# Gates and output projection of a hybrid decoder layer as seven block products in place of eight, token-major

## The chip, the core and the metric

The kernel runs on one core of one Trainium2 chip. The metric is the time of one execution on the device, in microseconds (us). The core has five engines that run side by side, each through its own list of instructions in order: TensorE (PE in the rows, with its weight loads as PEld), VectorE (DVE), ScalarE (ACT), GpSimd (POOL) and SyncE (SP), which here only issues DMA transfers. They wait for one another on semaphores. SBUF is the memory beside the engines, PSUM the eight banks that TensorE writes to.

## What is computed

One layer on 512 tokens of 2048 channels, all in float32. The parts that matter here:

```python
h = _rmsnorm(x, norm_g[l])
proj = jnp.einsum('bsd,df->bsf', h, w_in[l])      # 2048 x 24576
parts = jnp.split(proj, SPLIT_POINTS, axis=-1)
...                                               # attention A, attention B, short convolution C
gates = jax.nn.sigmoid(parts[9 + 3 * n_g] + gate_b[l]).reshape(bsz, seq, N_BRANCH, D_MODEL)
...
merged = (gates[:, :, 0] * jnp.einsum('bsw,wd->bsd', ya, w_branch_a[l])
          + gates[:, :, 1] * jnp.einsum('bsw,wd->bsd', yb, w_branch_b[l])
          + gates[:, :, 2] * jnp.einsum('bsw,wd->bsd', yc, w_branch_c[l]))
x = x + jnp.einsum('bsd,de->bse', merged, w_out[l])
return _rmsnorm(x, final_g)
```

18 x 1024 of the columns of `w_in` feed the three branches, the last 6144 the gates. `ya`, `yb`, `yc` are 1024 wide; `w_out` is 2048 x 2048.

## The kernel before

Everything lies channel-major in SBUF: 128 channels on the partitions, the 512 tokens along them. A weight **unit** is 128 x 1024 floats (512 KB): eight 128 x 128 blocks. TensorE multiplies in a rounded float32 format (fp32r), so each operand is split in a high part (`w_hi`, `act_hi`) and what is left (`w_lo`, `act_lo`), and a product is three matmuls (`three`, L329): high by high, low by high, high by low. A unit is thus 8 x 3 = 24 matmuls of a 128 x 128 stationary block of weights against 128 x 512 of activations, accumulated in one PSUM bank (`multiply`, L335).

The units pass through a ring of three slots. SyncE loads `raw[slot]` when the low part that was made from the slot before is done (semaphore `lo_done`); ScalarE copies it to `w_hi[slot]` (`split_hi`, L571), for which TensorE must have finished the unit three places earlier (`pe_used`); VectorE subtracts to get `w_lo[slot]` (`split_lo`, L811); TensorE waits for `lo_done` (L499 to L530). The order of the work is written out by hand: each engine's program says between which units its other instructions stand.

Four stages: the heads (8 heads x 36 units of `w_in`, with the attention and convolution work of that head between units; `y` of each branch is stored to DRAM); the merged columns (16 columns, each of six gate units and three branch units, `merge_block`, L499, `merge`, L1034), which are stored to DRAM, too; the output projection (16 blocks of two units, `out_block`, L525), the result read out of PSUM and added to `x` by `add_residual` (L1094); and the final norm, whose sum over channels is a sum over partitions, so it goes through GpSimd and two small turns on TensorE (L542 to L560) before all 16 blocks are scaled and stored.

Units: 288 + 96 + 48 + 32 = 464, so 464 x 24 = 11136 large matmuls.

## Time and profile before

| | |
|---|---|
| time of 3 runs | median 2722.65 us, 2722.07 to 2724.84 |
| the profiled execution | 2723.15 us, span 2721.4 us, mean granted clock of TensorE 0.997 |
| TensorE busy | 2690.2 us (99%) |
| VectorE, ScalarE, GpSimd busy | 1223.5 us (45%), 764.1 us (28%), 25.7 us (1%) |
| chain that ended last | TensorE 96%, VectorE 2%, DMA 1%, ScalarE 1% |
| DMA | 278.64 MB, mean 102 GB/s |

The rows come from one profiled execution. A row of the timeline gives start, duration, engine, line, operation, output<-inputs and shapes; the bracket is how long the engine stood idle before it and what ended that. Matmuls overlap: each row shows 0.39 us, but the next one starts 0.23 us later, so it is the distance of the starts that counts. The same holds by some tenths for VectorE and ScalarE.

### The profile page before, as it was taken

What the parts mean: (1) busy time and instruction counts of PE and PEld (TensorE: products, weight loads), DVE (VectorE), ACT (ScalarE), POOL (GpSimd) and SP (SyncE); (2) the same over time, 40 slices, a digit from 0 to 9 for tenths busy, and PEclk for the clock granted to TensorE, in tenths of its full rate; (3) what the DMA queues carried; (4) which work ended last, traced back from release to release, by engine and by line L of the source; (5) the groups of instructions that cost most, each with busy time, mean ns of one, the idle gap of its engine ahead of it and who ended that gap; (6) DMA issues with size and microseconds to landing.
All of it is one profiled execution on the core that took longest, in us unless ns stands there. A gap on an engine that the chain in (4) does not pass through costs nothing.

```text
span 2721.4 us, 32865 instructions
## 1 busy us (share of the span) xinstructions
PE 2690.2 (99%) x12330; PEld 2225.3 (82%) x12330; DVE 1223.5 (45%) x1613; ACT 764.1 (28%) x973; POOL 25.7 (1%) x23
## 2 busy tenths in 40 slices
PE   8999999999999999999999999999999999999997
PEld 6888888888888888888888888878888888888786
DVE  6554553554554455454455455443333333333323
ACT  5222322322232232232222232332222222223332
POOL 0000000000000000000000000000000000000011
PEclk9999999999999999999999999999999999999998
DMA  5222222222222222222222322443233333233532
GB/s 183 89 86 101 88 90 99 93 89 94 93 89 93 93 91 87 97 96 83 97 89 87 100 91 90 143 141 107 97 103 101 104 100 104 96 108 120 189 100 93
DMA packets 85119, 278.64 MB, mean 102 GB/s; under 512 B 9121, under 2 KB 9378, under 8 KB 85026
## 3 DMA queue, kind: packets, MB, share of 16 engines
q1 hardware_dynamic: 75472, 259.56, 28.7%
q10 hardware_dynamic: 9554, 17.63, 1.7%
q8 instruction: 83, 1.36, 0.2%
q14 instruction: 10, 0.08, 0.0%
HBM read 262.74 MB, written 14.42 MB: 102 GB/s over the span
## 4 chain that ended last, share of the span: by engine, by line
PE 96%; DVE 2%; DMA 1%; ACT 1%; issue 0%; DVEq 0%; ACTq 0%; SPq 0%
PE proj L331 30%; PE proj L333 30%; PE proj L332 30%; PE tr_ps L372 2%; PE sc_ps L364 1%; DMA raw<-wst 1%; PE o_ps L417 1%; PE sc_ps L403 1%; DMA raw<-y_dram 0%; DVE res L1120 0%; DVE y_lo L817 0%; PE o_ps L332 0%; PE o_ps L333 0%; PE o_ps L331 0%; PE sc_ps L332 0%
## 5 line engine op out<-in xcount | busy, mean ns | idle before, releaser
L331 PE MATMUL proj<-act_hi,w_hi 128*128 128x512 f32 x3328 | 1308.1, 393 | 10.9 <-DVE act_lo L826 8.7
L333 PE MATMUL proj<-act_hi,w_lo 128*128 128x512 f32 x3328 | 1297.3, 390 | 0.0
L332 PE MATMUL proj<-act_lo,w_hi 128*128 128x512 f32 x3328 | 1296.0, 389 | 0.0
L813 DVE TENSOR_TENSOR w_lo<-raw,w_hi 128x1024 fp32r<-128x1024 f32 x464 | 568.5, 1226 | 1001.8 <-ACT w_hi L575 1001.4
L575 ACT ACTIVATE w_hi<-raw 128x1024 fp32r<-128x1024 f32 x464 | 491.1, 1059 | 1404.9 <-PE proj L333 1383.4
L331 PEld LDWEIGHTS proj<-act_hi,w_hi 128*128 128x128 f32 x3328 | 625.5, 188 | 138.3 <-issue 11.7
L333 PEld LDWEIGHTS proj<-act_hi,w_lo 128*128 128x128 f32 x3328 | 625.2, 188 | 132.4
L332 PEld LDWEIGHTS proj<-act_lo,w_hi 128*128 128x128 f32 x3328 | 625.8, 188 | 126.5
L331 PE MATMUL proj<-y_hi,w_hi 128*128 128x512 f32 x384 | 150.0, 391 | 1.8 <-DVE y_lo L817 1.8
L332 PE MATMUL proj<-y_lo,w_hi 128*128 128x512 f32 x384 | 150.1, 391 | 0.0
L333 PE MATMUL proj<-y_hi,w_lo 128*128 128x512 f32 x384 | 150.0, 391 | 0.0
L613 ACT ACTIVATE sc<-sc,nmax 128x768 f32<-128x768 f32 (+4 forms) x96 | 65.5, 683 | 181.8 <-DVE nmax L898 101.9
L331 PEld LDWEIGHTS proj<-y_hi,w_hi 128*128 128x128 f32 x384 | 72.5, 189 | 17.3 <-issue 2.2
L333 PEld LDWEIGHTS proj<-y_hi,w_lo 128*128 128x128 f32 x384 | 72.5, 189 | 15.1
L332 PEld LDWEIGHTS proj<-y_lo,w_hi 128*128 128x128 f32 x384 | 72.4, 188 | 15.1
L884 DVE TENSOR_TENSOR stage<-proj,rstd 128x512 f32<-128x512 f32 x40 | 27.6, 691 | 100.3 <-PE proj L333 100.3
L627 ACT ACTIVATE qk_hi<-stage 128x512 fp32r<-128x512 f32 x32 | 20.2, 632 | 150.2 <-DVE stage L884 106.4
L688 ACT ACTIVATE gate<-gate,cols 128x512 f32<-128x512 f32 x48 | 34.8, 725 | 95.4 <-DVE gate L1042 95.4
L882 DVE TENSOR_TENSOR qk<-proj,rstd 128x512 f32<-128x512 f32 x32 | 34.5, 1079 | 57.5 <-PE proj L333 57.5
L882 DVE TENSOR_TENSOR stage<-proj,rstd 128x512 f32<-128x512 f32 x24 | 26.2, 1090 | 69.1 <-PE proj L333 69.1
L884 DVE TENSOR_TENSOR z<-proj,rstd 128x512 f32<-128x512 f32 x24 | 16.6, 692 | 73.7 <-PE proj L333 73.7
L372 PE MATMUL tr_ps<-ident,pr 128*128 128x128 f32 x272 | 41.0, 276 | 0.0
(135 smaller groups left out, 1151.3 us busy)
## 6 DMA issues: line engine op xcount, KB each, us to landing
raw<-wst SPq DMA_DIRECT2D x464, 512.0 KB, 3.3
raw<-y_dram SPq DMA_DIRECT2D x12, 512.0 KB, 3.7
y_dram<-y_b ACTq DMA_DIRECT2D x16, 256.0 KB, 2.6
res<-x_t ACTq DMA_DIRECT2D x1, 4096.0 KB, 19.8
m_dram<-gate ACTq DMA_DIRECT2D x15, 256.0 KB, 2.7
x_raw<-x_t SPq DMA_DIRECT2D x7, 512.0 KB, 9.2
raw<-m_dram SPq DMA_DIRECT2D x7, 512.0 KB, 3.8
out<-res ACTq DMA_DIRECT2D x12, 256.0 KB, 2.2
```

The lines of the kernel that those rows point to most:

```text
L331: nc.tensor.matmul(out, w_h, a_h, start=first, stop=False)
L332: nc.tensor.matmul(out, w_h, a_l, start=False, stop=False)
L333: return nc.tensor.matmul(out, w_l, a_h, start=False, stop=last)
L364: end = nc.tensor.matmul(sc_ps[m][:, 0:n], q_part[AQ][rows, qs], k_part[AK][rows, 0:n], start=step == 0, stop=step == 2)
L372: end = nc.tensor.transpose(tr_ps[idx % 2][:, n * P:(n + 1) * P], tile, ident[:, :])
L403: end = nc.tensor.matmul(sc_ps[1][:, (g - 1) * P:g * P], blk[q][:, qs], blk[k][:, qs], start=True, stop=True)
L575: nc.scalar.activation(w_hi[slot_w][:, :], raw[slot_raw][:, :], ACT.Copy).then_inc(hi_done, 1)
L613: end = nc.scalar.activation(tile[:, lo:hi], tile[:, lo:hi], ACT.Exp, scale=scale, bias=nmax[:, m:m + 1], accum_out=sums[:, m:m + 1])
L688: nc.scalar.activation(gate[b][:, :], gate[b][:, :], ACT.Tanh, scale=0.5, bias=col).then_inc(gate_done, 1)
L813: tt(w_lo[slot_w][:, :], raw[slot_raw][:, :], w_hi[slot_w][:, :].bitcast(f32), ALU.subtract).then_inc(lo_done, 1)
L882: ins = tt(as_class(blk[w][:, :]), by_class(pb[w % RING][:, :]), by_class(rstd[:, :]), ALU.mult)
L884: ins = tt(blk[w][:, :], pb[w % RING][:, :], rstd[:, :], ALU.mult)
```

## The change

The gates and the output projection are now made by a 2 x 2 block scheme with 7 products in place of 8 (Winograd's form). A **quad** is 1024 output columns: the result (512 tokens x 1024) is four blocks of 256 x 512, the activations four blocks of 1024 channels x 256 tokens, the weights four blocks `W11, W12, W21, W22` of 1024 x 512. Each of the seven products (L588) multiplies a sum of activation blocks by a sum of weight blocks, in `NU` = 4 **steps**; a step uses one ring slot of 128 x 1024 weights and is 2 token halves x 2 x 3 = 12 matmuls, so a quad is `STEPS` = 28 steps and 336 matmuls, where eight units of 24 x 2 were 384. Six quads make the gates, two the output projection. Of the seven weight operands three are blocks as they are and four are sums. In the gate stage VectorE makes the sums (`add_units`, L1019: four kinds, 16 instructions of 128 x 1024 per quad); those of `w_out` are made one unit per head while the heads run (`sum_out_units`, L1041), with 2 MB loaded and 2 MB stored on ScalarE's DMA queue each time (`s_dram`). The sums of activations are made once: eight instructions of 128 x 2048 between the blocks of the last head (`combine_h`, L1107), more at the start of the first gate quad and of the first output quad, each followed by a split (`comb_high`, `comb_low`).

The operands change places: the activations are now stationary, the weights stream, and the result lies token-major, 128 tokens on the partitions and 512 channels in a bank. So the scale 1/rms is a number per partition, and the bias a row broadcast by DMA (`rows`). Each product is read out of PSUM once (`take_g`, `take_o`; seven reads of two banks per quad). Gates go to DRAM (`g_dram`) and come back for the branches, which run after all gates: 12 groups of four units of 24 matmuls, four banks each (`take_group`, L1359). The merged result is then turned to channel-major by 64 fp32 transposes on TensorE (`turn_merged`, L621), the output quads use it, and the final norm is a sum along the row on ScalarE (`square_out`, with `accum_out`). GpSimd has no work left. The last head, the gates, the groups and the output are written out without loops.

```diff
-NBLK1, NBLK2, NBLK3 = 18, 6, 16
-NHU1, NHU2 = 36, 9
-W1 = HEADS * NHU1
-W2 = KT * NHU2
+W1 = HEADS * NHU1
+H, C = T // 2, 512
...
+QUADS_G, QUADS_O = 6, 2
+GROUPS, NU = 12, 4
+GIVES = [(0, 1, True), (3, -1, True), (1, 1, True), (0, 1, False), (3, -1, False), (1, 1, False), (2, -1, True)]
+LAST_OF = {0: 3, 3: 4, 1: 5, 2: 6}
+EVICT_AT = {6: 0, 10: 1, 14: 2, 18: 3, 22: 4, 26: 5}
+TANH_AT = {20: 0, 24: 3}
+S_ORDER = [2, 3, 0, 1]
+R1, R3, R2, R4 = range(4)
...
 # TensorE: the merged columns and the output blocks go, a product takes their place
-            def merge_block(evac, ready, y_needed=(0, 0, 0)):
-                for b in range(3):
-                    pe.wait_ge(evac_done, evac + (b + 1))
-                    for half in range(2):
-                        pe.wait_ge(lo_done, ready[2 * b + half])
-                        multiply(b, (2 * b + half) % RING, act_hi, act_lo, 8 * half, half == 0, half == 1)
-                for b in range(3):
...
-            def out_block(bank, slot, evac, ready):
-                pe.wait_ge(evac_done, evac + 1)
-                for half in range(2):
-                    for sem_, value in ready[half]:
-                        pe.wait_ge(sem_, value)
-                    multiply(bank, (slot + half) % RING, act_hi, act_lo, 8 * half, half == 0, half == 1)
...
+            def product(r, operand, banks, p, free=None, between=None):
+                hi, lo = operand
+                for u in range(NU):
+                    pe.wait_ge(lo_done, r + NU * p + u + 1)
+                    slot = (r + NU * p + u) % RING
+                    for s in range(2):
+                        if free and u == 0:
+                            pe.wait_ge(free[0], free[1][s])
+                        for kk in range(2):
+                            k, ts, cs = 2 * u + kk, slice(P * s, P * (s + 1)), slice(C * kk, C * (kk + 1))
+                            end = three(banks[s][:, :], hi[:, k, ts], lo[:, k, ts], w_hi[slot][:, cs], w_lo[slot][:, cs],
+                                        FRESH[p] and k == 0, k == 7, True)
...
+            def free_g(q, p):
+                if CHAIN[p] == ON_X:
+                    back = (q - 1, 5) if p == 0 else (q, {2: 0, 4: 2, 6: 4}[p])
+                elif CHAIN[p] == ON_Z:
+                    back = (q - 1, 3) if p == 1 else (q, 1)
+                else:
+                    back = (q - 1, 6)
+                return (got, [evicted(*back, s) for s in range(2)]) if back[0] >= 0 else None
...
+            def turn_merged(g, s):
+                cg = g % 4
+                pe.wait_ge(m_added, 4 * (g - 4) + spot(s) + 1)
+                for kk in range(4):
+                    end = nc.tensor.transpose(sets[g % 2][s][:, P * kk:P * (kk + 1)],
+                                              merged[:, s, C * cg + P * kk:C * cg + P * (kk + 1)], ident[:, :])
+                end.then_inc(m_turned, 1)
...
 # ScalarE: where the high part of step n comes from
+            def hi_g(q, n):
+                p, u = divmod(n, NU)
+                r = R_G + STEPS * q + n
+                if p == 0:
+                    act.wait_ge(k1_in[u], 16 * (q + 1))
+                    hi_of(r, k1[u])
+                elif p == 1:
+                    act.wait_ge(sum_done, summed(R1, q, u))
+                    hi_of(r, k2[u])
+                elif p == 2:
+                    act.wait_ge(sum_done, summed(R2, q, u))
+                    hi_of(r, k1[u])
+                elif p == 4:
+                    act.wait_ge(sum_done, summed(R3, q, u))
+                    hi_of(r, k3[u])
+                elif p == 5:
+                    act.wait_ge(sum_done, summed(R4, q, u))
+                    hi_of(r, k1[u])
+                else:
+                    hi_ring(r, 8 * q + (u if p == 3 else NU + u))
...
 # VectorE: sums of weight blocks, of W_out while the heads run, and the reads of PSUM
+            def add_units(kind, q, u):
+                if kind == R1:
+                    if u == 0:
+                        dve.wait_ge(k2_in, 16 * (q + 1))
+                        dve.wait_ge(k3_in, 16 * (q + 1))
+                    ins = tt(k2[u], k2[u], k3[u], ALU.add)
+                elif kind == R3:
+                    dve.wait_ge(k1_in[u], 16 * (q + 1))
+                    ins = tt(k3[u], k3[u], k1[u], ALU.add)
+                elif kind == R2:
+                    dve.wait_ge(sum_done, summed(R1, q, u))
+                    ins = tt(k1[u], k1[u], k2[u], ALU.add)
+                else:
+                    dve.wait_ge(sum_done, summed(R2, q, u))
+                    ins = tt(k1[u], k1[u], raw[(8 * q + u) % RING][:, :], ALU.add)
+                ins.then_inc(sum_done, 1)
...
+            def sum_out_units(i):
+                dve.wait_ge(osum_in, 16 * (i + 1))
+                link(tt(ssum[:, W22, :], ssum[:, W22, :], ssum[:, W21, :], ALU.add))
+                tt(ssum[:, W21, :], ssum[:, W21, :], ssum[:, W11, :], ALU.add)
+                link(tt(ssum[:, W11, :], ssum[:, W11, :], ssum[:, W22, :], ALU.add))
+                tt(ssum[:, W12, :], ssum[:, W12, :], ssum[:, W11, :], ALU.add).then_inc(osum_done, 1)
...
-            def merge(j, t, used, gates):
-                if t in (1, 3, 5):
-                    b = t // 2
-                    dve.wait_ge(pe_used, used)
-                    if b == 2:
-                        dve.wait_ge(m_stored, 16 * j + 16)
-                    tt(gate[b][:, :], pb[b][:, :], rstd[:, :], ALU.mult).then_inc(evac_done, 1)
...
+            def take_g(q, p):
+                d, sign, first = GIVES[p]
+                dve.wait_ge(pe_used, RING + R_G + STEPS * q + NU * (p + 1))
...
+                for s in range(2):
+                    b = 2 * (d % 2) + s
+                    scale = (rcol if sign > 0 else nrcol)[:, b:b + 1]
+                    bank, tile = pairs[(q + CHAIN[p]) % 3][s], gin[:, 2 * d + s, :]
+                    if first:
+                        if q:
+                            dve.wait_ge(g_stored[2 * d + s], 16 * q)
+                        other = rows[:, C * (d // 2):C * (d // 2 + 1)]
+                    else:
+                        dve.wait_ge(got, evicted(q, GIVES.index((d, sign, True)), s))
+                        other = tile
+                    stt(tile, bank[:, :], scale, other, ALU.mult, ALU.add).then_inc(got, 1)
...
 # VectorE, each gate block: what stands behind the low part of step n
+                    if q or n >= RING:
+                        lo_g(q, n)
+                    if q and n == 2:
+                        take_g(q - 1, 6)
+                    if n < 4:
+                        add_units(R3, q, n)
+                    if 4 <= n < 8:
+                        add_units(R2, q, n - 4)
+                    if 12 <= n < 16:
+                        add_units(R4, q, n - 12)
+                    if 24 <= n and q < QUADS_G - 1:
+                        add_units(R1, q + 1, n - 24)
+                    if q == 0 and n == 3:
+                        link(stt(f3, f2, -1.0, as_f32[11][0], ALU.mult, ALU.subtract))
+                        tt(f3, f3, as_f32[11][1], ALU.subtract).then_inc(comb_sum, 1)
+                    if q == 0 and n == 4:
+                        dve.wait_ge(comb_sum, 4)
+                        comb_low(t2[1], f2, t2[0], 2)
+                    if q == 0 and n == 8:
+                        comb_low(t4[1], f4, t4[0], 3)
+                    if q == 0 and n == 10:
+                        comb_low(t3[1], f3, t3[0], 4)
+                    if n in EVICT_AT:
+                        take_g(q, EVICT_AT[n])
+                    if q == QUADS_G - 1 and 17 <= n < 21:
...
+                    stt(to if b == 0 else tile, tile, 1.0, sets[g % 2][s][:, :], ALU.add, ALU.mult).then_inc(m_got, 1)
+                if b:
+                    for s in S_ORDER:
+                        tile, to = gin[:, 4 * (g % 2) + s, :], merged[:, s, C * cg:C * (cg + 1)]
+                        dve.wait_ge(m_got, 4 * g + spot(s) + 1)
+                        if b == 2:
+                            dve.wait_ge(m_added, 4 * (g - 8) + spot(s) + 1)
+                        tt(to, to, tile, ALU.add).then_inc(m_added, 1)
...
 # SyncE: when a slot of raw is free
+            def ring_free(x):
+                if x < RING:
+                    sp.wait_ge(lo_done, W1 - RING + x + 1)
+                elif x < X_B + RING:
+                    q, n = divmod(x - RING, 8)
+                    if n < NU:
+                        sp.wait_ge(sum_done, summed(R4, q, n))
+                    else:
+                        sp.wait_ge(lo_done, R_G + STEPS * q + 24 + n - NU + 1)
+                else:
+                    sp.wait_ge(lo_done, R_B + x - RING - X_B + 1)
...
```

Where the instructions stand. **VectorE at the end of the last head.** Before, directly behind the last head's `y_b<-cc,z`:

```order
L817 TENSOR_TENSOR y_lo<-raw0,y_hi 128x1024
L813 TENSOR_TENSOR w_lo0<-raw1,w_hi0 128x1024
L817 TENSOR_TENSOR y_lo<-raw2,y_hi 128x1024
L817 TENSOR_TENSOR y_lo<-raw0,y_hi 128x1024
L813 TENSOR_TENSOR w_lo1<-raw1,w_hi1 128x1024
L1042 TENSOR_TENSOR gate0<-proj0,rstd 128x512
```

After, the same place, from just ahead of the last head's last two splits (`kb` holds weight blocks and their sums, `tb_f` the sums of activations, `z<-proj2` is the last read of a head's block, `y_b` its result):

```order
L1025 TENSOR_TENSOR kb<-kb 128x1024 x4
L1011 TENSOR_TENSOR w_lo1<-kb,w_hi1 128x1024
L1127 TENSOR_TENSOR tb_f<-tb_f,act_lo 128x2048
L1138 TENSOR_TENSOR z<-proj2,rstd 128x512
L1011 TENSOR_TENSOR w_lo2<-kb,w_hi2 128x1024
L1201 SCALAR_TENSOR_TENSOR z<-th,z 128x512
L1291 SCALAR_TENSOR_TENSOR y_b<-cc,z 128x512
L1028 TENSOR_TENSOR kb<-kb 128x1024 x3
L1011 TENSOR_TENSOR w_lo0<-kb,w_hi0 128x1024
L1028 TENSOR_TENSOR kb<-kb 128x1024
L1345 SCALAR_TENSOR_TENSOR act_lo_f<-tb_f,act_hi 128x8x256
L1346 TENSOR_TENSOR act_lo_f<-act_lo_f,act_lo 128x8x256
```

What moved: the splits of `y` are gone from here; four sums stand ahead of the split of step 1, a sum of activations ahead of the last read of the head, four sums ahead of and behind the split of step 3 (`w_lo0`), and two sums of activations ahead of the split of step 4.

**VectorE at the start of the output projection.** Before, the last splits of the merged stage and the first two of the output:

```order
L813 TENSOR_TENSOR w_lo2<-raw0,w_hi2 128x1024
L1085 TENSOR_TENSOR act_lo<-raw1,act_hi 128x512
L1091 TENSOR_TENSOR act_lo<-gate2,act_hi 128x512
L813 TENSOR_TENSOR w_lo0<-raw2,w_hi0 128x1024
L813 TENSOR_TENSOR w_lo1<-raw0,w_hi1 128x1024
L1098 SCALAR_TENSOR_TENSOR res<-proj0,res 128x512
```

After, from step 6 of the first quad (`kb<-kb,tb_f` is a sum of merged blocks, `kb_r` and `act_hi` take low parts, L1404 adds a product to `x` in `act_lo_f`; the program's names are those of the memory, so the low part of o21 reads act_hi):

```order
L1429 SCALAR_TENSOR_TENSOR kb<-kb,tb_f 128x2048
L1011 TENSOR_TENSOR w_lo1<-raw1,w_hi1 128x1024
L1039 TENSOR_TENSOR kb_r<-kb,kb_r 128x2048
L1011 TENSOR_TENSOR w_lo2<-raw2,w_hi2 128x1024
L1039 TENSOR_TENSOR act_hi<-tb_f,act_hi 128x2048
L1011 TENSOR_TENSOR w_lo0<-raw0,w_hi0 128x1024
L1404 SCALAR_TENSOR_TENSOR act_lo_f<-sc_ps0,act_lo_f 128x512
L1404 SCALAR_TENSOR_TENSOR act_lo_f<-sc_ps1,act_lo_f 128x512
L1011 TENSOR_TENSOR w_lo1<-raw1,w_hi1 128x1024
L1404 SCALAR_TENSOR_TENSOR act_lo_f<-tr_ps0,act_lo_f 128x512
L1404 SCALAR_TENSOR_TENSOR act_lo_f<-tr_ps1,act_lo_f 128x512
L1011 TENSOR_TENSOR w_lo2<-raw2,w_hi2 128x1024
```

What moved: sums and splits of 128 x 2048 stand between the steps, and the first product is read out of `sc_ps` only behind the split of step 9.

**TensorE, one step.** Before, the start of a unit of a head; the gate units read alike, with 24 such rows to one bank:

```order
L331 MATMUL proj1<-act_hi,w_hi0 128x512
L332 MATMUL proj1<-act_lo,w_hi0 128x512
L333 MATMUL proj1<-act_hi,w_lo0 128x512
L331 MATMUL proj1<-act_hi,w_hi0 128x512
L332 MATMUL proj1<-act_lo,w_hi0 128x512
L333 MATMUL proj1<-act_hi,w_lo0 128x512
L331 MATMUL proj1<-act_hi,w_hi0 128x512
```

After, step 0 of the first gate quad:

```order
L419 MATMUL sc_ps0<-w_hi0,act_hi 128x512
L420 MATMUL sc_ps0<-w_lo0,act_hi 128x512
L421 MATMUL sc_ps0<-w_hi0,act_lo 128x512
L419 MATMUL sc_ps0<-w_hi0,act_hi 128x512
L420 MATMUL sc_ps0<-w_lo0,act_hi 128x512
L421 MATMUL sc_ps0<-w_hi0,act_lo 128x512
L419 MATMUL sc_ps1<-w_hi0,act_hi 128x512
L420 MATMUL sc_ps1<-w_lo0,act_hi 128x512
L421 MATMUL sc_ps1<-w_hi0,act_lo 128x512
L419 MATMUL sc_ps1<-w_hi0,act_hi 128x512
L420 MATMUL sc_ps1<-w_lo0,act_hi 128x512
L421 MATMUL sc_ps1<-w_hi0,act_lo 128x512
```

What moved: twelve matmuls in place of 24 use one ring slot, and the bank changes after six.

## Rows read from the trace of the kernel before

**Rows 1.** the page: the span, then the busy time of each engine and its share
```profile
span 2721.4 us, 32865 instructions
...
PE 2690.2 (99%) x12330; PEld 2225.3 (82%) x12330; DVE 1223.5 (45%) x1613; ACT 764.1 (28%) x973; POOL 25.7 (1%) x23
```

**Rows 2.** what TensorE (PE) waited for, whole span: us in total, times, longest us
```profile
PE proj L331 <- DVE act_lo L1091: 2.2, 1, 2.2
...
PE proj L331 <- DVE y_lo L817: 1.8, 1, 1.8
```

**Rows 3.** stretches: busy us of each engine, granted clock, DMA share, GB/s
```profile
1800.00:2400.00 600.00, 600.00 (x2648) 496.81 (x2647) 195.20 (x207) 143.53 (x147) 0.00 (x0) 1.00 0.31 102
2535.00:2540.00 5.00, 5.00 (x23) 4.14 (x23) 0.00 (x0) 1.01 (x1) 0.00 (x0) 1.00 1.04 406
```

**Rows 4.** TensorE in order of time, inside the gate stage
```profile
2152.72 0.39 PE L331 MATMUL proj<-act_hi,w_hi 128*128 128x512 f32 x1
...
2157.93 0.39 PE L333 MATMUL proj<-act_hi,w_lo 128*128 128x512 f32 x1
```

**Rows 5.** TensorE at the first matmuls of the program
```profile
9.65 0.63 PE L333 MATMUL proj<-act_hi,w_lo 128*128 128x512 f32 x1
...
12.21 0.63 PE L333 MATMUL proj<-act_hi,w_lo 128*128 128x512 f32 x1
```

**Rows 6.** TensorE around six fp32 transposes of one head
```profile
194.41 0.81 PE L372 MATMUL tr_ps<-ident,pr 128*128 128x128 f32 x6
194.98 0.48 PE L331 MATMUL proj<-act_hi,w_hi 128*128 128x512 f32 x1
195.29 0.39 PE L332 MATMUL proj<-act_lo,w_hi 128*128 128x512 f32 x1
```

**Rows 7.** ScalarE (ACT) and VectorE (DVE) in the same stretch as rows 4
```profile
2155.64 1.06 ACT L575 ACTIVATE w_hi<-raw 128x1024 fp32r<-128x1024 f32 x1 [4.38 <-PE proj L333]
...
2156.73 1.23 DVE L813 TENSOR_TENSOR w_lo<-raw,w_hi 128x1024 fp32r<-128x1024 f32 x1 [4.21 <-ACT w_hi L575]
2157.87 0.69 DVE L1042 TENSOR_TENSOR gate<-proj,rstd 128x512 f32<-128x512 f32 x1
```

**Rows 8.** VectorE, two reads of PSUM back to back
```profile
1704.17 0.68 DVE L931 TENSOR_TENSOR pt_lo<-tr_ps,pt_hi 128x512 fp32r<-128x512 f32 x1
1704.77 0.42 DVE L937 COPY pt_g<-tr_ps 128x256 f32<-128x256 f32 x1
```

**Rows 9.** groups by line and shape: busy us, mean ns of one | idle before, releaser
```profile
L813 DVE TENSOR_TENSOR w_lo<-raw,w_hi 128x1024 fp32r<-128x1024 f32 x464 | 568.5, 1226 | 1001.8 <-ACT w_hi L575 1001.4
...
L754 ACT ACTIVATE rsq<-res 128x512 f32 x9 | 5.7, 632 | 17.9 <-DVE res L1098 17.9
```

**Rows 10.** VectorE from the last head into the first gate block
```profile
1732.68 0.69 DVE L1018 TENSOR_TENSOR cc<-cc,cb 128x512 f32<-128x512 f32 x1
1734.16 1.23 DVE L813 TENSOR_TENSOR w_lo<-raw,w_hi 128x1024 fp32r<-128x1024 f32 x1 [0.79 <-ACT w_hi L575]
1738.51 0.69 DVE L884 TENSOR_TENSOR z<-proj,rstd 128x512 f32<-128x512 f32 x1 [3.12 <-PE proj L333]
```

**Rows 11.** ScalarE at the start of the output projection
```profile
2538.99 1.06 ACT L575 ACTIVATE w_hi<-raw 128x1024 fp32r<-128x1024 f32 x1 [5.76 <-DMA raw<-wst]
```

**Rows 12.** DMA issues by line: count, KB each, median us to landing
```profile
raw<-wst SPq DMA_DIRECT2D x464, 512.0 KB, 3.3
...
res<-x_t ACTq DMA_DIRECT2D x1, 4096.0 KB, 19.8
...
out<-res ACTq DMA_DIRECT2D x12, 256.0 KB, 2.2
```

**Rows 13.** end of the program: TensorE's last product, then VectorE
```profile
2701.66 0.39 PE L333 MATMUL proj<-act_hi,w_lo 128*128 128x512 f32 x1
...
2702.08 0.69 DVE L1098 SCALAR_TENSOR_TENSOR res<-proj,res 128x512 f32<-128x512 f32 x1 [10.19 <-PE proj L333]
...
2706.99 11.57 DVE L1120 TENSOR_TENSOR res<-res,frstd 128x512 f32<-128x512 f32 x12 [1.88 <-ACT frstd L780]
```

More of the change, by code:

```diff
@@ L773, in _ @@
[L773 to L783 removed]
+            head(HEADS - 1)
@@ L1154 @@
     wi = [units(w_in, half) for half in range(2)]
-    wb = [units(get(f"w_branch_{x}")[0], 0) for x in "abc"]
-    wo = [units(get("w_out")[0], half) for half in range(2)]
     nb = HEADS
```

941 lines of the change are left out of this document (571 added, 370 removed).

## The prediction

> **What bounds the kernel now.** I read the page first: TensorE is busy for 2690.2 of 2721.4 us [rows 1]. Then what it waited for: inside the program there are two waits, 2.2 and 1.8 us; the rest of its idle time lies ahead of its first and behind its last matmul [rows 2]. In the stretch from 1800 to 2400 us it never stops, while VectorE works 195.2 and ScalarE 143.5 of the 600 us and the transfers run at 102 GB/s [rows 3]. So the time is the number of matmuls by their distance. From 2152.72 to 2157.93 there are 23 distances, across the border of a unit (ScalarE's `w_hi` at 2155.64 marks it): 0.2267 us each, 5.44 us a unit [rows 4, 7]. The 390 ns that a row shows overlap and are not the price.
>
> What a unit waits for: ScalarE starts the high part when TensorE has left the slot, 1.09 us on VectorE starts the low part, which takes 1.23 us, and VectorE is free for its next instruction 1.14 us after the start [rows 7]. So a low part is there 2.5 us after the unit two places ahead began, and is needed two units after that start. At 5.44 us a unit the slack is 8.4 us; at the new 2.72 us a step it is 5.44 - 2.5 = 2.9 us. The change leaves the bound where it is and cuts the slack to a third.
>
> **The change part by part.** The sum is made on the span, 2721.4 us.
>
> 1. Matmuls. Gates and output were 96 + 32 units of 24; they become 8 quads of 28 steps of 12. 3072 - 2688 = 384 fewer, by 0.2267: **-87.1 us**. The branches keep 1152 matmuls, the heads all theirs. The form is the same before and after, 128 x 128 stationary against 128 x 512, so I take the same distance. The bank now changes after six matmuls and not after 24 or 48.
>
> 2. Transposes, 64 of fp32. Six take from 194.41 to 194.98, and the matmul behind them is 0.31 us from its follower and not 0.23 [rows 6]: 0.57 + 0.08 for six, so 0.10 to 0.11 each, in eight or fewer bursts: **+7.4 us**. Nothing hides them, they are on TensorE.
>
> 3. The two waits of 2.2 and 1.8 us are on splits of what had come back from DRAM [rows 2]. Both go. The new first output product needs groups 8 and 9 of the merged result, turned two groups (43 us) earlier; `y` of branch A is split 7 steps before it is used: **-4.0 us**.
>
> 4. The regular gate quads. VectorE has per quad 28 low parts and 16 sums of the same size at 1.14 us, and 14 reads of PSUM at 0.60 (the distance in [rows 8]): 58.6 us of 76.2. The densest stretch is step 24 to step 7 of the next quad, with a sum behind every step: 12 x 2.28 + 3 x 1.2 = 31.0 us against 12 x 2.72 = 32.6. It keeps up, and the slack of 2.9 us covers the reads: **0**. At the full durations (1.226 and 0.69 us [rows 7, 9]) it is 33.6 against 32.6, still within the slack; that cover gone, each quad costs 1 to 4 us. ScalarE has 28 x 1.06 us and 8 tanh of 0.7: far from full.
>
> 5. The first gate quad has three times that work in front. T is the end of the last head's last matmul. VectorE is done with the convolution at T - 5.2 (1733.3 against 1738.5 [rows 10]). Four sums to T - 0.6, low part of step 1 to 0.6, a sum of 128 x 2048 to 2.8. 512 columns take 0.69 and 1024 take 1.23 us [rows 7], so 2048 take 2.3 and free the engine after 2.2. Then the last head's read 3.4, low part of step 2 4.6, silu and `y_b` 6.1, three sums 9.5, low part of step 3 at 10.7. TensorE wants it at 8.2: wait of 2.5. A sum of weights and two of 2.2 us bring the low part of step 4 to 17.5, where TensorE was ready at 13.4: 4.1. Carried on in the same way: 1.8 at step 5, 0.4 at step 7, 0.4 more by step 11, then VectorE gets ahead. **+9.2 us**. If VectorE starts earlier or the instructions are shorter, 4; if each wait is dearer than its row, 14.
>
> 6. The first output quad. The merged blocks are summed and split there: nine instructions of 2.2 us between steps 6 and 17. The first product's banks are read out behind step 9's low part. With step 0 at 0 and the transposes behind steps 2 and 3, TensorE reaches step 8 at 23.9 and needs the first of these banks; VectorE, held by three large instructions (14.3 to 16.6, 19.1 to 21.3, 22.5 to 24.7) and the low part of step 9 (25.8), has read it at 26.4: wait of 2.5. Steps 13, 14 and 16 come 0.4, 0.6 and 0.3 late. **+3.8 us**. At the same time `x` is loaded, 4 MB. When this was done before, the whole ran at 406 GB/s [rows 3] and a ring load made ScalarE stand for 5.8 us [rows 11]: it landed some 7.8 us after its slot was free, not the usual 3.3 [rows 12]. In the new ring a load has 3 x 2.72 us less the 2.5 of the splits until ScalarE wants it, then the slack of 2.9: 8.5 us. Just enough for 7.8; I add **+1.2**. Bounds of the two together: 0 and 15.
>
> The Trainium skill, "DMA: Bandwidth & Descriptors", section on queues, rings and completion order, says each DMA engine takes turns between the queues that have work. By that the ring would keep half of 406 GB/s, 2.6 us for a unit, under the 2.72 of a step, and the 1.2 would be 0. The trace's one stall of this kind is what I keep.
>
> 7. The heads. Four sums of 1024 per head come in where VectorE stood idle for over 3 us ahead of a read of PSUM, with units of 5.44 us behind: 4.6 us, of which 1.4 delay that read by less than the slack. The same for one large instruction per block of the last head. The 2 + 2 MB per head are 34 MB over 1700 us, 20 GB/s beside some 92. **0**; if it is not hidden, up to 1 us a head.
>
> 8. The end. Before, 19.7 us lay between the start of the last product and the end of the span: a read, squares, two turns over TensorE until 2706.99, 16 scalings (12 of them 11.6 us on VectorE) and stores of 2.2 us [rows 12, 13]. Now three blocks of four are squared before that point. Left are two reads (to 1.8), two squares of 0.63 (2.8) [rows 9], three small column operations (3.6 to 4), scalings by 512 and 1536 columns (6) and a last store of 768 KB, with 1 MB still ahead of it: 2 us and the time of the bytes at 300 to 400 GB/s, so 11 to 12. **-8 us**, bounds -4 and -11.
>
> Sum: 2721.4 - 87.1 + 7.4 - 4.0 + 9.2 + 5.0 - 8.0 = 2643.9. The profiled execution was 2723.15, 1.75 over its span, and 0.5 over the median of the runs. So 2643.9 + 1.3 = **2645 us**, 0.971 of before.
>
> **Rivals.**
> - *Slower: the ring becomes the bound.* A slot goes round in landing + 1.09 + 1.23 + some 0.1. At 3.3 us landing that is 5.7 for three steps of 8.2; at the 7.8 us seen next to a large load it is 10.2, 3.40 us a step. The output quads ask for 512 KB per 2.72 us, 193 GB/s, and the gate quads for some 143 with 2 MB bursts among them, against 102 before. All 224 steps at 3.40 would cost 152 us: 2797 us. It decides from 3.07 us a step, a landing of 6.8 us. Against it: 406 GB/s were reached [rows 3], and 3.3 us holds for 464 loads [rows 12].
> - *VectorE is late in every quad.* If its work in the dense stretch takes a fifth more than the distances say (37 us for 32.6, less 2.9 slack), each later gate quad loses 2 us and the first two quads of their kind a third more: +15, 2660 us. For it: the margin in point 4 is 1.6 us. Against: the rows' durations hardly spread.
> - *The distance grows.* If each change of bank costs the 0.08 us seen behind the transposes [rows 6], then 448 changes in the quads and some 190 in the branches give +51 us, 2696 us. Against: across the unit border of [rows 4] nothing is lost.
> - *The clock falls in the waits of point 5.* The first matmuls of the program stand 0.427 us apart, the pace of 1.2 GHz [rows 5]; if three waits in 15 us bring that back for 22 matmuls, +4.4 us: 2650. After the wait of 2.2 us the pace did not fall: 23 matmuls in the next full 5 us [rows 3]. The Trainium skill, "TensorE: Matmul & The Clock Gate", section on psum-queue depth-cycling, describes a kernel that went through PSUM banks and idled briefly between groups so often that the clock swung between its levels; by that rule the quads, with their banks changing every six matmuls, would be the place. In this trace only a wait makes a gap, not a bank.
> - *No saving at all*, the products keeping 8/8 of the work, is excluded: the order of the instructions shows 12 matmuls a step.
>
> **How the numbers follow.** The forecast, with its own range 2631 (points 5 and 6 at zero, 2721.4 - 87.1 + 7.4 - 4 - 8 + 1.3) to 2660, has 0.68. VectorE late in every quad 0.15, the clock 0.08, the distance 0.05, the ring 0.04. The range reaches over the first three: 2630 to 2672. A difference of 0.2% (5.4 us) is about what can be told from none here. Only the ring lies on the other side or near it: faster 0.96, same 0.01, slower 0.03.
>
> **What would show it.** TensorE with 10,752 large matmuls at 0.227 and 64 transposes; its waits inside the program 14 us, two thirds of them at steps 3 to 5 of the first gate quad on `w_lo`, one of 2.5 us at step 8 of the first output quad on a read of PSUM; none over 1 us in the later gate quads; the median landing of the ring under 4.5 us; under 12 us from the last product to the end. The prediction is wrong if the distance is not 0.227, or if waits on `w_lo` return in each quad.

## The result, and the profile after

The changed kernel takes 2645.95 us (median of 4 runs, 2645.44 to 2650.81), the kernel before 2723.39 beside it (2722.07 to 2724.84): a ratio of 0.972, 95% interval 0.9703 to 0.9736. The forecast was 2645. The profiled execution is the longest of the four, 2650.81 us; the spans of the others are 2643.7 to 2644.3, where the sum of the forecast had 2643.9.

The page, to be read beside [rows 1]: 344 records of TensorE fewer (384 - 64 = 320 by the program; a trace lacks some), and VectorE at 59% in place of 45%.

```profile
span 2649.0 us, 31176 instructions
...
PE 2617.0 (99%) x11986; PEld 2161.9 (82%) x11986; DVE 1554.4 (59%) x1910; ACT 866.9 (33%) x1089; POOL 0.2 (0%) x4
```

What TensorE waited for, beside [rows 2] (us in total, times, longest). `w_lo` L1011 are low parts of weights, `act_lo_f` L1404 a read of an output bank:

```profile
PE proj L419 <- DVE act_lo L1055: 8.1, 1, 8.1
PE tr_ps L419 <- DVE w_lo L1011: 2.5, 1, 2.5
PE sc_ps L419 <- DVE w_lo L1011: 2.5, 1, 2.5
PE sc_ps L419 <- DVE act_lo_f L1404: 2.4, 1, 2.4
PE sc_ps L452 <- DVE qk_lo L1196: 2.2, 1, 2.2
PE sc_ps L419 <- issue: 1.5, 1, 1.5
PE tr_ps L529 <- DVE xacc L1065: 1.0, 1, 1.0
PE proj L419 <- DVE w_lo L1011: 0.9, 2, 0.6
```

The places are the forecast ones: 2.5 at step 3 and 2.5 at step 4 of the first gate quad, 2.4 at step 8 of the first output quad, 0.9 at its steps 13 and 14. The 1.5 us at the start of the branches was not forecast. Together these are 9.8 us where I had said 14; the rest came in another form, next.

Stretches (length, then busy us of TensorE, its weight loads, VectorE, ScalarE, GpSimd, the granted clock, DMA share, GB/s). The last runs from step 10 of the first gate quad into the sixth: TensorE never stops, though it changes its bank every six matmuls. The first three lie around the waits:

```profile
1750.00:1760.00 10.00, 6.01 (x20) 4.22 (x18) 9.96 (x8) 6.06 (x6) 0.00 (x0) 0.83 0.07 26
1760.00:1770.00 10.00, 8.99 (x32) 7.04 (x33) 10.00 (x10) 3.77 (x3) 0.00 (x0) 0.83 0.00 0
2500.00:2510.00 10.00, 7.60 (x27) 5.81 (x26) 7.11 (x9) 3.18 (x3) 0.00 (x0) 0.83 1.00 399
1780.00:2200.00 420.00, 419.96 (x1853) 347.42 (x1852) 336.36 (x322) 190.93 (x203) 0.00 (x0) 1.00 0.48 165
```

TensorE at step 3 of the first gate quad. Behind the wait the matmuls stand 0.427 us apart, as in [rows 5], then 0.23 again: the granted clock fell to its lower level, 1.2 GHz, for some 3 us.

```profile
1751.24 0.39 PE L421 MATMUL sc_ps<-w_hi,act_lo 128*128 128x512 f32 x1
1754.09 0.79 PE L419 MATMUL sc_ps<-w_hi,act_hi 128*128 128x512 f32 x1 [2.46 <-DVE w_lo L1011]
1754.69 0.63 PE L420 MATMUL sc_ps<-w_lo,act_hi 128*128 128x512 f32 x1
1755.11 0.63 PE L421 MATMUL sc_ps<-w_hi,act_lo 128*128 128x512 f32 x1
...
1757.17 0.40 PE L420 MATMUL sc_ps<-w_lo,act_hi 128*128 128x512 f32 x1
1757.40 0.39 PE L421 MATMUL sc_ps<-w_hi,act_lo 128*128 128x512 f32 x1
```

The end, beside [rows 13]: 11.1 us from the start of the last matmul to the end of the span, before it was 19.7.

```profile
2637.90 0.39 PE L421 MATMUL proj<-w_hi,kb_r 128*128 128x512 f32 x1
2638.33 0.69 DVE L1404 SCALAR_TENSOR_TENSOR act_lo_f<-o_ps,act_lo_f 128x512 f32<-128x512 f32 x1 [2.66 <-PE proj L421]
...
2642.48 1.01 DVE L1477 TENSOR_SCALAR act_lo_f<-act_lo_f,fcol 128x1536 f32<-128x1536 f32 x1
```

The ring's median landings over the whole program are 3.3 to 4.0 us, before 3.3 [rows 12].

### The profile page after: what moved, and what is told of

Its sections match the earlier page's. It is cut to its first block, busy times and chain, and to the rows that moved or that the text cites. A ratio compares the mean times of both kernels' runs of the same rounds, so it can differ in the third digit from the quotient of the medians.

```text
span 2649.0 us, 31176 instructions
## 1 busy us (share of the span) xinstructions
PE 2617.0 (99%) x11986; PEld 2161.9 (82%) x11986; DVE 1554.4 (59%) x1910; ACT 866.9 (33%) x1089; POOL 0.2 (0%) x4
## 4 chain that ended last, share of the span: by engine, by line
PE 96%; DVE 3%; SPq 0%; DMA 0%; ACT 0%; issue 0%; DVEq 0%; ACTq 0%
PE proj L419 22%; PE proj L421 22%; PE proj L420 22%; PE sc_ps L419 3%; PE sc_ps L421 3%; PE sc_ps L420 3%; PE tr_ps L419 3%; PE tr_ps L421 3%; PE tr_ps L420 3%; PE o_ps L420 2%; PE o_ps L421 2%; PE o_ps L419 2%; PE tr_ps L460 2%; PE sc_ps L452 1%; PE o_ps L505 1%; PE sc_ps L491 1%
## 5 line engine op out<-in xcount | busy, mean ns | idle before, releaser
L419 PE MATMUL proj<-act_hi,w_hi 128*128 128x512 f32 x2304 | 910.9, 395 | 8.1 <-DVE act_lo L1055 8.1
L421 PE MATMUL proj<-act_hi,w_lo 128*128 128x512 f32 x2304 | 900.4, 391 | 0.0
L420 PE MATMUL proj<-act_lo,w_hi 128*128 128x512 f32 x2304 | 899.8, 391 | 0.0
L419 PEld LDWEIGHTS proj<-act_hi,w_hi 128*128 128x128 f32 x2304 | 434.3, 189 | 96.4 <-issue 9.0
L421 PEld LDWEIGHTS proj<-act_hi,w_lo 128*128 128x128 f32 x2304 | 434.1, 188 | 92.1
L420 PEld LDWEIGHTS proj<-act_lo,w_hi 128*128 128x128 f32 x2304 | 434.7, 189 | 86.9
L1011 DVE TENSOR_TENSOR w_lo<-raw,w_hi 128x1024 fp32r<-128x1024 f32 x152 | 185.7, 1223 | 220.6 <-ACT w_hi L702 220.6
L702 ACT ACTIVATE w_hi<-kb 128x1024 fp32r<-128x1024 f32 x120 | 127.2, 1061 | 185.2 <-PE proj L421 64.4
L1011 DVE TENSOR_TENSOR w_lo<-kb,w_hi 128x1024 fp32r<-128x1024 f32 x120 | 146.5, 1222 | 57.7 <-ACT w_hi L702 57.7
L419 PE MATMUL tr_ps<-w_hi,act_hi 128*128 128x512 f32 x192 | 74.7, 389 | 0.0
L420 PE MATMUL tr_ps<-w_lo,act_hi 128*128 128x512 f32 x192 | 74.7, 389 | 0.0
```

The lines of the kernel that those rows point to most:

```text
L419: nc.tensor.matmul(out, w_h, a_h, start=first, stop=False, skip_group_check=shared)
L420: nc.tensor.matmul(out, w_h, a_l, start=False, stop=False, skip_group_check=shared)
L421: return nc.tensor.matmul(out, w_l, a_h, start=False, stop=last, skip_group_check=shared)
L702: nc.scalar.activation(w_hi[r % RING][:, :], src, ACT.Copy).then_inc(hi_done, 1)
L1011: tt(w_lo[r % RING][:, :], src, w_hi[r % RING][:, :].bitcast(f32), ALU.subtract).then_inc(lo_done, 1)
```

## The experiments

"Excess" below is the time between the starts of TensorE's matmuls in a stretch, less 0.2267 us for each: waits and slow matmuls together, a few tenths rough. The control was timed together with e2, e3 and e4; the other kernels were timed later, with the kernel before at 2723.17 (e5, e6, e7_one_more, e9) and 2722.64 us (e7_two_more, e8, e10) where it had 2722.17 beside the control. So their differences from the control may be off by some 1 us through that alone.

**e0_same**, the control.

> The changed kernel, unaltered, as the measure for the kernels beside it: 2645 to 2646 us. In its profiled execution the waits on w_lo at steps 3 and 4 of the first gate quad are again 2.5 us each and the one at step 8 of the first output quad 2.4 us. If the 5 us that the opening of the first profiled execution lost (matmuls 0.427 us apart behind the waits at 39 and 51 us) belong to the kernel, they are there again; if they belong to that execution, they are not.

2646.92 us (2645.61 to 2649.61). The waits are 2.46 at step 3 and 3.86 at step 4, as the forecast's 2.5 and 4.1; here the clock fell only behind the second:

```profile
1757.33 0.77 PE L419 MATMUL tr_ps<-w_hi,tb 128*128 128x512 f32 x1 [3.86 <-DVE w_lo L1011]
1757.89 0.63 PE L420 MATMUL tr_ps<-w_lo,tb 128*128 128x512 f32 x1
...
1762.59 0.48 PE L419 MATMUL tr_ps<-w_hi,tb 128*128 128x512 f32 x1
```

The excess of the quad is 9.5 us in both executions, whatever the clock did. In the first, slow matmuls of step 3 took the place of wait at step 4; in both, those behind the wait of step 4 took the place of the waits forecast for later steps. In the opening 8 matmuls are slow here, 18 in the first profile.

**e2_sums_spread**, VectorE's work in the first gate quad in another order (core of the edit):

```
-                if w == 17:
-                    tt(f4, f4, as_f32[21][1], ALU.subtract).then_inc(comb_sum, 1)
+                    if q == 0 and n == 16:
+                        tt(f4, f4, as_f32[21][1], ALU.subtract).then_inc(comb_sum, 1)
...
-                    if 4 <= n < 8:
-                        add_units(R2, q, n - 4)
+                    r2_at = (4, 7, 8, 9) if q == 0 else (4, 5, 6, 7)
+                    if n in r2_at:
+                        add_units(R2, q, r2_at.index(n))
...
-                    if q == 0 and n == 3:
+                    if q == 0 and n == 5:
                         link(stt(f3, f2, -1.0, as_f32[11][0], ALU.mult, ALU.subtract))
```

> In the first gate quad VectorE's sums are put in another order: the second instruction of f4 and its low part go to steps 16 and 20, the pair for f3 from step 3 to step 5, the low part of t2 from step 4 to step 7, and the sums of weights R2 to steps 4, 7, 8 and 9. Nothing is taken away. Theory (VectorE's chain is what TensorE waits for in the first gate quad): the waits at steps 3 to 5 shrink from 5.0 us and the matmuls at 0.427 behind them to about 3.7 us together, 5 to 6 us come off the time: 2640. Rival (what is late there are the loads of the quad, landing beside the 4 MB for its sums): the order of VectorE's work changes nothing, 2645 to 2646. Second rival (the low clock makes the loss, and any wait over 1 us brings it): one or two waits of 1 to 2 us stay and bring back 3 us of slow matmuls, 2643.

2640.17 us (2640.07 to 2641.48), 6.7 under the control. The excess of the quad is 4.1 us in place of 9.5. TensorE's waits there:

```profile
PE tr_ps L419 <- DVE w_lo L1011: 1.7, 1, 1.7
...
PE sc_ps L419 <- DVE w_lo L1011: 0.3, 1, 0.3
```

and 1.2 at step 8, behind the low part of `t2`. None of these brought the low clock. The loads were the same, so they were not what was late; VectorE's chain was.

**e3_y_before_ring**

```
+                if q == QUADS_G - 1:
+                    sp.wait_ge(ylo_done, 4)
+                    load_y(1)
                 load_22(q, 3)
-            sp.wait_ge(ylo_done, 4)
-            load_y(1)
```

> SyncE issues the 2 MB load of y for branch B before the last load of the last gate quad, some 15 us earlier, and no longer just ahead of the first three weight units of the branches. Theory (the 1.5 us that TensorE stood at the start of the branches is the first weight unit, behind those 2 MB in the queue): the wait goes, 1.5 to 1.7 us less, 2644. Rival (the profile calls the wait 'issue', so it is TensorE's own change from one loop's code to the next): it stays, 2645 to 2646, and the first weight unit is there early.

2643.9 us (2643.67 to 2645.65), 3.0 under the control by medians and 1.9 by the lowest. The wait is gone, excess 0.0 in place of 1.8. ScalarE at the first weight unit of the branches, first in the control, then here:

```profile
2205.40 1.06 ACT L702 ACTIVATE w_hi<-raw 128x1024 fp32r<-128x1024 f32 x1 [6.11 <-DMA raw<-wb]
```

```profile
2200.73 1.06 ACT L703 ACTIVATE w_hi<-raw 128x1024 fp32r<-128x1024 f32 x1 [1.66 <-PE proj L422]
```

So the line "issue" was a DMA: the 2 MB of `y` ahead of 512 KB in one queue.

**e4_read_first**

```
                         if n == 8:
-                            comb_low(o21[1], m21, o21[0], 8)
-                        if n == 9:
                             take_o(0, 0)
+                            comb_low(o21[1], m21, o21[0], 8)
```

> In the first output quad VectorE reads the first product's banks out in step 8, ahead of the 2.2 us low part of the merged block and of the low part of step 9, and not behind both. Theory (TensorE waits at step 8 for these banks): the wait of 2.4 us goes, and with it the matmuls at 0.427 us behind it; the delay is given back in part at steps 13 and 14, where VectorE's sums of the merged blocks are late: 2.5 to 4 us less, 2642. Rival (the load of x, 4 MB, holds up the ring here, and the bank is only where it shows): the wait moves to a w_lo of steps 8 to 10, 0 to 1 us less, 2645.

2646.58 us (2645.7 to 2648.42), 0.3 under the control: the theory missed, and the rival's 0 to 1 us less holds, but not its place. The wait at step 8 went, and one of the same length came at step 13. VectorE and TensorE there:

```profile
2505.46 2.28 DVE L1439 TENSOR_TENSOR gin<-tb_f 128x2048 f32<-128x2048 f32 x1
2507.67 1.22 DVE L1011 TENSOR_TENSOR w_lo<-raw,w_hi 128x1024 fp32r<-128x1024 f32 x1
2508.80 2.28 DVE L1442 TENSOR_TENSOR kb<-gin,tb_f 128x2048 f32<-128x2048 f32 x1
2511.12 2.29 DVE L1443 TENSOR_TENSOR kb<-kb,tb_f 128x2048 f32<-128x2048 f32 x1
2513.33 1.22 DVE L1011 TENSOR_TENSOR w_lo<-raw,w_hi 128x1024 fp32r<-128x1024 f32 x1
```

```profile
2511.60 0.39 PE L421 MATMUL proj<-w_hi,act_hi 128*128 128x512 f32 x1
2514.60 0.50 PE L419 MATMUL proj<-w_hi,act_hi 128*128 128x512 f32 x1 [2.61 <-DVE w_lo L1011]
```

Three sums of 128x2048 stand between the low parts of steps 11 and 13. VectorE did not work without a break up to there. It stood idle before the low parts of steps 10 and 11, whose high parts came late because ScalarE had waited for ring loads issued beside the load of `x` (the last row is ScalarE ahead of step 11):

```profile
2500.57 1.23 DVE L1011 TENSOR_TENSOR w_lo<-raw,w_hi 128x1024 fp32r<-128x1024 f32 x1 [1.13 <-ACT w_hi L702]
2504.32 1.23 DVE L1011 TENSOR_TENSOR w_lo<-raw,w_hi 128x1024 fp32r<-128x1024 f32 x1 [1.33 <-ACT w_hi L702]
```

```profile
2503.23 1.06 ACT L702 ACTIVATE w_hi<-raw 128x1024 fp32r<-128x1024 f32 x1 [2.69 <-DMA raw<-s_dram]
```

So much of the time that the early read gained VectorE spent waiting for the ring, and TensorE paid at the end of the chain, at step 13. In this run the rival has a part in it; e4 alone can't tell it from the length of VectorE's work, e5 can.

**e5_all**, e2, e3 and e4 together, and those sums moved apart (the low parts of `m22` and `g4f` go two steps later, too):

```
-                    if q == 0 and n == 11:
+                    if q == 0 and n == 9:
                         tt(g3f, m22, m12, ALU.subtract).then_inc(comb_sum, 1)
-                    if q == 0 and n == 12:
+                    if q == 0 and n == 11:
...
+                    if q == 0 and n == 16:
                         tt(g4f, g4f, m21, ALU.subtract).then_inc(comb_sum, 1)
```

> The order of the first gate quad from the run with the sums spread, the early load of y, and in the first output quad a new order of VectorE's work: the first product's banks are read in step 8, the sum g3f comes at step 9, the two instructions of g4f at steps 11 and 16, the low parts of m22 and g4f at steps 17 and 19. Theory (all the excess outside the opening is VectorE's chain at these two places and the first branch unit): the excess of the first output quad falls from about 7 us, waits and slow matmuls together, to about 1.5, since ScalarE's wait for the ring beside the load of x stays; the branches start without a wait: 2640.2 - 1.8 - 4 = 2634 to 2636. Rival (the time lost in the output quad is conserved, as when only the read was moved, because the ring beside the load of x sets it): 2638 to 2639.

2635.55 us (2635.03 to 2637.52), 0.968 of before, interval 0.9666 to 0.9693, and 11.4 us under e0_same. The excess of the output quad fell from 6.3 (with e4) to 2.0: two waits on `w_lo` of 0.2 and 0.3 and one of 0.5, no slow matmul. The ring loads beside `x` landed as late as in the control (8.8, 7.8 and 8.4 us, there 9.3, 8.3 and 7.4), so late loads by themselves do not make the excess: with the large sums spread over more steps it is gone. This version beats both kernels.

**e10_r1_earlier**, in `head`, on top of e5_all:

```
-                    if last and w == 17:
+                    if last and w == 16:
                         for n in range(NU):
                             add_units(R1, 0, n)
```

> The kernel of the last run with all three repairs, and in it the four sums R1 of the first gate quad (4.6 us of VectorE) one block earlier, into the 6 us in which VectorE stands idle behind y_b of branch B; the 4 MB that they add have landed by then. Theory (the 3.9 us that the first gate quad still loses are the length of VectorE's chain, whatever its order): they go, 2631 to 2632. Rival (the chain is held at steps 4 and 8 by the loads of k1 and the low part of t2, and not by its length): 2634 to 2636.

2636.2 us (2634.74 to 2638.36): the same as e5_all, excess 4.0 in place of 4.1. The sums ran in the idle time, and VectorE then stood idle where they had been:

```profile
1718.97 4.62 DVE L1026 TENSOR_TENSOR kb<-kb 128x1024 f32<-128x1024 f32 x4
...
1736.00 1.23 DVE L1012 TENSOR_TENSOR w_lo<-kb,w_hi 128x1024 fp32r<-128x1024 f32 x1 [0.86 <-ACT w_hi L703]
1740.22 0.69 DVE L1137 TENSOR_TENSOR z<-proj,rstd 128x512 f32<-128x512 f32 x1 [2.99 <-PE proj L422]
...
1743.84 3.49 DVE L1029 TENSOR_TENSOR kb<-kb 128x1024 f32<-128x1024 f32 x3
```

The chain that binds begins at 1740.22 with the read of the last head's last block, which TensorE releases; from there to the wait at step 8 VectorE stands idle only once, for 0.46 us. My reason for the gain was wrong; the rival's places (steps 4 and 8) fit, but its cause was not tried. Moving the three sums R3 (3.5 us, at 1743.84) was not tried either.

**e6_eighth_back**

```
+                            for again in range(2 if p == 3 else 1):
+                                end = three(banks[s][:, :], hi[:, k, ts], lo[:, k, ts], w_hi[slot][:, cs], w_lo[slot][:, cs],
...
```

> Product 3 of every quad issues its 48 matmuls twice (its banks then hold the double, so this part of the result is not the reference's): 384 matmuls of 128 x 512 more, nothing else added. Theory (the saving is 384 matmuls by 0.2267 us and nothing else that the change did): 87 us more, less 1 us for the two short waits at steps 13 and 14 of the first output quad, for which there is now time: 2732 to 2734. Rival (in the quads the transfers or VectorE hold the pace, and the eighth product would lie beside them): 40 us or less more.

2734.15 us (2729.8 to 2734.89), 87.2 over the control by medians and 84.2 by the lowest runs: 384 matmuls are worth 384 x 0.2267 = 87.1 to within the spread of the runs, and that the medians agree to 0.1 is chance. The two waits of steps 13 and 14 are gone, as expected, while the wait at the start of the branches is 1.9.

**e9_turned_twice** (`for kk in [0, 1, 2, 3] * 2` in `turn_merged`).

> Each of the 64 transposes is issued twice into the same place. Theory (they lie on TensorE's own path, 0.105 to 0.11 us each, hidden by nothing): 7 us more, 2653. Rival (at the first output quad TensorE waits for VectorE anyway, so the 16 more of group 11 only shorten that wait): 5 us more. Rival (the profile's distances between transposes are not their price): 0 to 3, or over 12 us.

2653.59 us (2651.55 to 2658.33), 6.7 over the control, 0.104 us for each transpose, or 5.9 by the lowest runs: between the first two expectations. In the changed kernel's trace sixteen of them take 1.66 us from 2441.86, and 0.08 behind.

**e7_one_more** and **e7_two_more**, a loop of 1 or 2:

```
+                    if 24 <= n and q < QUADS_G - 1 or n < 8 and q:
...
+                            link(tt(rows[:, 2 * C:3 * C], rows[:, 3 * C:4 * C], rows[:, 3 * C:4 * C], ALU.add))
```

> VectorE gets one more instruction of 128 x 512 fp32, waited for (0.7 us), in each of the 12 steps from step 24 of a gate quad to step 7 of the next, at all five crossings: 60 in all, 42 us of VectorE's time. Theory (the dense stretch has 32.6 us for 31.0 us of work and 2.9 us of slack): 8.4 us more at a crossing, of which 4.5 are free: 3.9 us at each of five, 19 us more, 2665, with waits on w_lo in every later gate quad. Rival (VectorE is at its limit there already): 42 us more, 2688. Rival (VectorE has room, since it is busy 0.8 of these quads): 0 to 3 us more.

> Two more instructions of 128 x 512 on VectorE, not one, in each of the 12 steps around every crossing of gate quads. With one, VectorE's period was 3.00 us a step, TensorE had the same, and a crossing cost 4.8 us. Theory (VectorE's chain sets TensorE's pace there): 12 x 0.71 = 8.5 us more at each of five crossings, all of it on the path: 2670.6 + 42.5 = 2713. Rival (the waits give VectorE room that it did not have): under 30 us more than with one. Second rival (waits every step bring the low clock): over 55 us more.

2670.61 us (2668.38 to 2670.69), 23.7 over the control, 4.7 a crossing and not 3.9; and 2714.42 us (2712.41 to 2718.04), 43.8 more. VectorE with one more, where the next step begins 3.00 us after the one before:

```profile
2079.22 1.22 DVE L1011 TENSOR_TENSOR w_lo<-kb,w_hi 128x1024 fp32r<-128x1024 f32 x1
2080.37 1.22 DVE L1031 TENSOR_TENSOR kb<-kb 128x1024 f32<-128x1024 f32 x1
2081.50 0.68 DVE L1358 TENSOR_TENSOR rows<-rows 128x512 f32<-128x512 f32 x1
2082.22 1.22 DVE L1011 TENSOR_TENSOR w_lo<-kb,w_hi 128x1024 fp32r<-128x1024 f32 x1
```

12 x 0.72 = 8.6 us were added and 4.7 paid, so a crossing has some 3.9 us of room; the next 8.6 are paid in full (8.8). The rival that VectorE was already at its limit is out. Behind the waits of 1.3 us with one more, no matmul was slow. With two more, 8 or 9 were slow behind a wait at four places, and the 8.8 a crossing leave little room for a price of theirs: VectorE sets the pace there, and TensorE only arrives later at its next wait.

**e8_half_copy** and **e8_ring_traffic**, in the output quads, behind each ring load, rows 0:64 or all of:

```
+                    sp.dma_start(x_dram[STEPS * q + n, :, :], wst[STEPS * q + n, :, :]).then_inc(x_copied, 16)
```

> Behind each of the 56 ring loads of the output quads the same queue copies 256 KB from DRAM to DRAM, which nothing waits for until the end. The quads then ask for 768 KB a step, 289 GB/s, or 385 if a copy counts for its read and its write. Theory (the ring binds only from a landing of 6.8 us, 3.07 us a step): the landing rises to 5 or 6 us, the time stays within 3 us of 2646. Rival (the ring is near its limit already, as the forecast's slower case had it): waits for raw in every step, 15 us or more.

> The same with 512 KB copied behind each load: 385 GB/s asked for, or 578 if a copy counts twice. Theory (over some 400 GB/s the queue backs up, a step then takes what its bytes take, and the landing is three steps less 2.5 us): counted twice, 3.87 us a step and a landing near 9 us, 64 us more, 2710; counted once, a landing of 6 to 7 us and 0 to 10 us more. Rival (the prefetch of three slots hides it): 0.

2647.73 us (2646.97 to 2648.86) and 2651.49 us (2649.03 to 2652.96). With the half copy the landings are 4.9 and 5.3 us, as its theory has it. With the full copy, the stretch from 2540 to 2600, the landings from 2480 to 2640, and what ScalarE waited for there:

```profile
2540.00:2600.00 60.00, 60.00 (x266) 49.67 (x266) 39.60 (x43) 27.03 (x34) 0.00 (x0) 1.00 1.00 385
```

```profile
raw<-s_dram SPq DMA_DIRECT2D x30, 512.0 KB, 5.7
raw<-wo SPq DMA_DIRECT2D x20, 512.0 KB, 5.9
```

```profile
ACT w_hi L705 <- DMA raw<-s_dram: 47.3, 29, 3.3
ACT w_hi L705 <- DMA raw<-wo: 27.2, 19, 3.2
```

The 385 GB/s are what was asked for, copies counted once, and TensorE never stops. ScalarE waits for almost every unit. The 6.8 us of my expectation is not where the ring begins to bind: by the forecast's own sum a slot goes round in landing + 1.09 + 1.23 + 0.1, which fills three steps of 2.72 at a landing of 5.7 us; 6.8 is where all that the change saves would be gone (224 steps x 0.35 = 78 us). So the full copy brought the steady steps to the edge and not past it. The trace agrees: the low parts are ready 0.5 to 2.6 us ahead of their step, without copies 2.9.

Past the edge the ring was in one place, the first output quad beside the load of `x`. With the full copy six loads in a row landed there in 9.2 to 10.1 us and were issued 3.6 to 4.3 us apart (the sum gives 4.1 for 10.0). The excess of that quad is 9.0, in the control 7.6 and in the first profile 6.1, with one wait of 2.6 us at a step of product 3. That is 1.4 to 2.9 of the 4.6 us between the medians; the rest was not found.

## Why the prediction was right, point by point

1. Matmuls, -87.1: shown, 87.2 (84.2 by the lowest runs) by putting them back, with their distance unchanged in the trace. The distance did not grow with the bank changes; that rival is false.
2. Transposes, +7.4: 0.104 to 0.109 us each, 6.7 to 7.0.
3. The two waits, -4.0: mis-sized, -5.9. My reading that these were TensorE's only waits inside the program was wrong: a third, of 2.2 us on `qk_lo`, stands at 48.41. The change leaves it (2.2 us in the changed kernel, too), so it is not in the difference. The two went, and with them something that I had not read. In the kernel before, the 1.8 us wait stands at 1783.80, and behind it eight matmuls 0.40 to 0.43 us apart, in a stretch granted 0.83. I had looked only behind the wait of 2.2 us, where the clock stayed up, and argued from it that it would. The two stretches of the kernel before, then TensorE in the first:

```profile
1780.00:1790.00 10.00, 8.19 (x29) 6.33 (x28) 6.12 (x8) 3.83 (x4) 0.00 (x0) 0.83 0.78 258
2530.00:2540.00 10.00, 7.80 (x35) 6.19 (x34) 3.60 (x4) 4.21 (x5) 0.00 (x0) 1.00 0.94 324
```

```profile
1783.80 0.47 PE L331 MATMUL proj<-y_hi,w_hi 128*128 128x512 f32 x1 [1.81 <-DVE y_lo L817]
...
1784.82 0.63 PE L332 MATMUL proj<-y_lo,w_hi 128*128 128x512 f32 x1
1785.25 0.63 PE L333 MATMUL proj<-y_hi,w_lo 128*128 128x512 f32 x1
```

4. Regular gate quads, 0: TensorE is busy 419.96 of 420 us; the room is 3.9 us a crossing and not 4.5, the value that the expectation of e7_one_more drew from the forecast.
5. First gate quad, +9.2: 9.5. The waits at steps 3 and 4 are 2.5 and 3.9 in the control; the rest came as slow matmuls and not as waits.
6. First output quad, +5.0: 6.0, and 7.6 in the control. The waits (2.4, 0.6, 0.3) fit. Slow matmuls behind the wait of 2.4 us cost 1.5: in e9 the wait was 2.35, no matmul was slow, and the excess 4.6 and not 6.1. For the load of `x` I had 1.2. The five ring loads beside it landed in 6.9 to 8.3 us, near the 7.8 of the forecast. In the first profile that cost nothing, since VectorE was still busy when the high part of step 9 came. In the control the load behind that high part landed in 9.3 us and not 8.0, VectorE stood idle for it, and the wait at step 8 was 3.1 and not 2.4. ScalarE, then VectorE, in the control:

```profile
2498.11 1.06 ACT L702 ACTIVATE w_hi<-raw 128x1024 fp32r<-128x1024 f32 x1 [2.43 <-DMA raw<-s_dram]
```

```profile
2499.20 1.23 DVE L1011 TENSOR_TENSOR w_lo<-raw,w_hi 128x1024 fp32r<-128x1024 f32 x1 [0.62 <-ACT w_hi L702]
```

7. Heads, 0: from the same instruction of the first head (past its opening) to that of the last it is 1507.18 us after and 1507.33 before.
8. End, -8: -8.6.

Not in the sum: +1.8 at the start of the branches. This is the one term that the forecast left out: I had counted the load of `y` as moved and not asked what stood behind it in SyncE's queue.

With the measured sizes: 2721.4 - 87.1 + 7.0 - 5.9 + 9.5 + 6.0 + 1.8 - 8.6 = 2644.1, where three executions had 2643.7 to 2644.3. The errors are +1.8, +1.0 and +0.3 against -1.9, -0.4 and -0.6: that the total is nearer than its terms is luck, and 1.9 and 1.8 are not related. The other three executions left no trace; that they had these sizes is not shown.

The profiled execution has 5 us more, and its opening has them: the same matmul behind the opening starts at 112.93, before at 107.73, with one more wait of 1.0 us and 18 slow matmuls (some 4 us). Up to that wait, at 38.81, the change alters no more than one small operation of VectorE at the start. Still, a wait of 0.2 to 1.3 us at that place stands in eleven of thirteen profiles of the changed kernels and not in the one profile of the kernel before. Whether part of it belongs to the change stays open.

The rivals. The ring: in the steady steps not reached, with 385 GB/s it came to its edge and did not bind; beside the load of `x` it cost nothing in the first profile and 0.7 us in the control. VectorE late in every quad: false, with 3.9 us to spare. The clock: it did fall, but in the first gate quad that cost nothing, since TensorE then arrived later at a wait that ended when VectorE was done; where it cost something was the output quad (1.5 us), which I had not priced.

The Trainium skill, "TensorE: Matmul & The Clock Gate", section on psum-queue depth-cycling, speaks of a kernel that went through PSUM banks with frequent short idle gaps between its groups of matmuls and saw its clock swing. The trace agrees that gaps can bring the low clock and shows that changing banks does not: 420 us of bank changes every six matmuls at 1.00, and 0.83 in the 10 us around a single wait. The skill's "DMA: Bandwidth & Descriptors", section on queues, rings and completion order, has each DMA engine take turns between the queues that have work, from which I had drawn half of the rate for the ring. The trace does not show a half: from 2492 to 2508, beside `x`, the ring's queue moved 2.15 of 6.28 MB, a third, with two or three loads in flight. Why is open.

## What to carry to other kernels

When the unit of work gets shorter, price the slack that the helper engine loses, and then walk its queue at the few places where one-off work piles up: that found every place in the quads, and missed the one wait that another queue made, SyncE's. A late chain is paid for at its end. Moving one instruction ahead of another only moved the wait (e4), and shortening the chain ahead of the event that restarts it gave nothing (e10), so find where the chain begins, and what holds it up on its way, before cutting it. Beside each wait in a trace, look at the pace of the matmuls behind it: it is part of what the wait costs.
